# A two-block transformer on one core: conditioning begun three steps sooner, products formed tile by tile behind two norms, and the final norm split in two

## The chip, the core and the metric

The kernel runs on one core of a Trainium2 chip. The metric is the device time of one execution in microseconds (us), shown as the median of three runs. A profile of one execution gives the span from the first to the last instruction and the rows quoted below. Lines such as L823 are those of the kernel before; PE is TensorE, PEld its weight loads, DVE VectorE, ACT ScalarE, POOL GpSimd, SP the queue that issues nearly all DMAs.

## What is computed

Two layers of a first block (three kinds of attention, then a gated FFN) are followed by a second block: an adaptive norm, a mixer of two linear-attention branches over 512 latent and 256 context tokens, a gated FFN, and a last norm. Width is 1024, FFN width 2816, all fp32. What the change touches:

```
mod   = silu(c) @ w_ada + b_ada          # 48 tiles of 128 features; 16 of them for the context too
u     = norm1(x) * (1 + sc1) + sh1       # latent, 512 tokens; u_c likewise for 256 context tokens
q, k, v, low_rank, gate, ... = split(u @ w_in), split(u_c @ w_in)
x     = x + g1 * mixer(...)
h     = norm2(x) * (1 + sc2) + sh2
x     = x + g2 * ((silu(h @ wa) * (h @ wb)) @ w_out)
out   = x * rsqrt(mean(x*x, features) + eps) * final_g
```

## The kernel before

The five engines each run a program written out by hand; semaphores alone order them. The stream `xT` is kept transposed, as 8 tiles of 128 features by 512 tokens. Exact fp32 products are three fp32r products: a value is split into a rounded high part and the rest, and high x high, low x high and high x low are summed in one PSUM bank. So a group over 8 feature tiles is 24 matmuls. ACT makes the high parts of weights and activations, DVE the low parts (POOL in a few places).

**FFN steps.** Each FFN has 38 steps `q` (`ffn`, `load_ffn`, `ffn_silu`, `ffn_sums`). Steps 0 to 21 form one tile of gate and one of up, 48 matmuls; steps 22 to 37 form half of one output tile each, 33 matmuls (the down stage). Weights go through two buffers: SP loads `raws`, ACT rounds it to `wH` (L1792), DVE subtracts to `wL` (L2289). SP issues the load of step `q` when step `q-2` is split.

**Conditioning.** `mod` needs 64 loads of `w_ada`, 32 in each of the first block's two FFNs, one per step from step `ADA_FIRST` = 5 to step 36. For each, SP loads 512 KB into one half of `spare` (L1506) behind the step's weights, and waits first until ACT has read the result before the last. POOL multiplies and folds the tile, PE sums it with two one-column matmuls behind the step's products, and ACT copies the column into `mod` (L1834) behind its split of the step after next. Two loads of the context tokens (L1540) wait for the last two results.

**Start of the second block.** ACT forms the root; DVE spreads it, and makes the 8 tiles of `u` one after another (L2267, L2270, then the low part L2263, with ACT's high part between them). PE first transposes the normed context (L1226), then forms the 32 low-rank rows of `u` tile by tile as the tiles come, and after them q and k of the first head, 24 matmuls each. ACT takes the context's banks between its high parts (L1856, L1857: 16 of them, scale and shift). The context's low parts are on DVE (L2337). Then come the context's low-rank rows, its k, the two decay products, six v tiles and two gate tiles. ACT evacuates in that order; between the decay products and the first v tile it does the decay's logarithms and exponentials, waiting for DVE's sums between them. The banks for these products are a ring of three.

**Second block's FFN.** Its norm is made in the same way. Step 0 forms the gate tile as the 8 tiles come, and then the up tile.

**End.** After the last down step, the squares (summed by POOL) give the mean; ACT takes the root, DVE inverts and spreads it through a matmul, and multiplies the 8 tiles by gain and inverse (L2062). PE transposes them back in 32 pieces (L1462), ACT copies eight banks to SBUF (L608) and issues one DMA of 2 MB.

Of the kernel before, what the change touches and what calls it, by code (L numbers as in the profile page):

```python
# [6 lines left out]
F32 = mybir.dt.float32  # L7
ALU = mybir.AluOpType
# [13 lines left out]
FT = FF // P  # L22
# [59 lines left out]
def build(nc, A, out):  # L82
    ctx = ExitStack()
    with ctx:
# [326 lines left out]
        sc_ready, st_ready = sem("sc_ready"), sem("st_ready")  # L411
        gates_logged = sem("gates_logged")
        og_ready, og_root, og_normed, y_ready = sem("og_ready"), sem("og_root"), sem("og_normed"), sem("y_ready")
        head_in = sem("head_in")
# [187 lines left out]

        def finish_act(act, ap, ab, f):
            ysb = R[:, 14208:14208 + TT * D].rearrange("p (t c) -> p t c", t=TT)
            for t in range(TT):
                for half in range(2):
                    bank = ab.take(act)
                    ap.do(f(ysb[:, t, half * 512:(half + 1) * 512], bank[:, :], ACT.Copy), a_free)  # L608
            act.dma_start(out[0].rearrange("(t p) c -> p t c", p=P), ysb).then_inc(out_done, 16)

# [4 lines left out]
        def _(pool):  # L615
# [187 lines left out]
            first_low(L)  # L803
            fold_squares()


        @block.tensor
        def _(pe):
# [303 lines left out]
            def ffn(l):  # L1112
# [24 lines left out]
                for q in range(NF):  # L1137
# [5 lines left out]
                    else:  # L1143
                        pe.wait_ge(wl_ready, g)
                    if q < FT:
                        for n, b_ in ((0, ab), (1, db)):
                            w = [(lambda k, t=t: t[:, g % 2, (n * KT + k) * P:(n * KT + k + 1) * P]) for t in (wH, wL)]
                            deferred = l < L and n == 0
                            bank = gate_bank(q) if deferred else b_.fill(pe)
                            products(bank[:, :], w, lambda k: xH[:, k, :], xl, list(range(KT)), True, True,  # L1150
                                     (lambda k: pp.more(xn_ready)) if q == 0 and n == 0 else None
                                     ).then_inc(gate_full if deferred else b_.filled, 1)
                            if l < L and q == 0:
                                if n == 0:
# [21 lines left out]
                if l == L - 1:  # L1176
                    folded_sums(PTb[:, 0, :], PTb[:, 1, :])
                elif l == L:
                    folded_sums(X(0), X(KT - 1))
                if l < L:  # L1180
# [38 lines left out]

            spread_roots(S)  # L1220
            pp.more(ctx_ready, CT)
            for kp in range(4):
# [125 lines left out]
            parts_job(ab, lambda b: b[0:32, 0:256], small(LR_AT, 2 * RANK), XcP)  # L1348
            pe.wait_ge(tab_in, 80)
            ranked = ab.n  # L1350
# [104 lines left out]
            ffn(L)  # L1455
            spread_roots(S)
            pp.more(xn_ready, KT)
            for t in range(TT):
                for half in range(2):
                    bank = ab.fill(pe)  # L1460
                    for f in range(4):
                        ins = nc.tensor.transpose(bank[:, f * P:(f + 1) * P], xn[:, half * 4 + f, t * P:(t + 1) * P], ident[:, :])  # L1462
                    ins.then_inc(a_full, 1)


        @block.sync
        def _(sp):
# [91 lines left out]
            load_ffn(L)  # L1559
            sp.wait_ge(out_done, 16)  # L1560


        @block.scalar
        def _(act):
# [229 lines left out]
            def second_ffn_inputs():  # L1794
# [7 lines left out]
                split_high(L, 1)  # L1802

            def ffn_silu(l):
                for q in range(NF):
# [14 lines left out]
                    if q >= FT and (q - FT) % 2:  # L1820
                        k = (q - FT) // 2
                        if l + 1 < L:
                            high_tile(x_high(k), k)
                        if l < L:
                            square_in_turn(k)
                        else:
                            square(k)
                    if l + 1 < L and q == NF - 2:
# [21 lines left out]
            for k in range(KT):  # L1850
                high_tile(x_high(k), k)
                if k % 2 == 0:
                    bank = ab.take(act)
                half = bank[:, k % 2 * 256:(k % 2 + 1) * 256]
# [3 lines left out]
                if k % 2:  # L1858
                    ap.also(ctx_split)

            def rank_rows(a, n):
# [66 lines left out]
            evacuate(0, *[("v", m) for m in range(4)])  # L1928
            evacuate(0, ("v", 4), ("v", 5), ("gate", 0), ("gate", 1))
            for h in range(NH2):  # L1930
# [75 lines left out]
            for n in range(2 * KT):  # L2006
# [4 lines left out]
                ap.also(gate_ready)  # L2011
            second_ffn_inputs()
            ffn_silu(L)
            root()
            finish_act(act, ap, ab, f)


        @block.vector
        def _(dve):
# [198 lines left out]

            def gained(k, gain):
                vp.do(v.tensor_scalar(Pb[:, k % 2, :], xT[:, k, :], gain(k), None, ALU.mult), scaled)  # L2220

# [79 lines left out]
            def ffn_sums(l, add):  # L2301
                for m in range(KT):
# [11 lines left out]
                    if l < L:  # L2314
                        fold(m)

# [15 lines left out]

            norm_into_parts(lambda k: gm[:, 0, k:k + 1], lambda k: mod[:, sh1 + k, 0:1], u_low, x_high, context_root)
            vp.more(ctx_split, KT // 2)
            for k in range(0, KT, 2):
# [5 lines left out]
            vp.do(v.memset(seg[:, 0:SEQ2:CH], 0.0))  # L2341

            def second_low(name, h):
                j = SECOND.index((name, h))
                raw_, high, low = place_parts(PLACE[j])
                dve.wait_ge(second_high, j)
                vp.do(v.tensor_tensor(low, raw_, high.bitcast(F32), ALU.subtract), piece_split)  # L2347

# [57 lines left out]

            second_low("v", 0)
            decay_sums(0, 0)
# [148 lines left out]
            for m in range(KT):  # L2557
# [5 lines left out]
                vp.also(x_ready)  # L2563
            ffn_norm(L, lambda k: gm[:, 2, k:k + 1], lambda k: mod[:, sh2 + k, 0:1])
            ffn_products(L)
# [58 lines left out]
```

## Time and profile before

| | |
|---|---|
| median of 3 runs (lowest, highest) | 2967.97 us (2957.62, 2972.18) |
| profiled execution | 2958.03 us |
| its span | 2956.2 us |
| mean granted TensorE clock in the span | 0.958 of full speed |
| PE busy in the span | 2765.4 us (94%) |
| chain that ended last, by engine | PE 76%, DVE 8%, ACT 7%, DMA 7% |

Times in the rows count from the start of the span. The profiled execution lies at the low end of the three runs. PE holds most of the chain, so the places of interest are those where another engine or a DMA holds it.

### The profile page before, as it was taken

How to read it: one execution, taken by the hardware profiler on the slowest of the kernel's cores; microseconds unless marked ns; L12 is line 12 of the kernel's file. 1: busy time of each engine (PE TensorE's matmuls, PEld its weight loads, DVE VectorE, ACT ScalarE, POOL GpSimd, SP SyncE). 2: the span in 40 equal slices, each digit the busy share in tenths (PEclk: the TensorE clock that was granted, in tenths of full speed). 3: DMA queues.
4: the chain of work that ended last, by engine and by line, in shares of the span. 5: the costliest groups of instructions: out<-in, count | busy, mean ns of one | idle time of the engine just before them, and what ended most of it. 6: DMA issues, size and time to landing. Idle time of an engine off the chain costs nothing.

```text
span 2956.2 us, 35461 instructions
## 1 busy us (share of the span) xinstructions
PE 2765.4 (94%) x13958; PEld 2144.4 (73%) x13958; DVE 1315.1 (44%) x1765; ACT 977.6 (33%) x1648; POOL 900.0 (30%) x664
## 2 busy tenths in 40 slices
PE   7989999999999799999998999898988999899997
PEld 7866658887798575788876776657776665688886
DVE  2758435453345773554424355645443112333322
ACT  5469522222253882222224334332222100222221
POOL 5566402435547551124463100300000322200000
PEclk8999999999999999999999999899987999899999
DMA  5230024554522101345453111011111331233332
GB/s 129 90 69 1 19 57 120 144 141 132 143 84 78 36 1 47 100 117 140 132 148 97 45 43 43 29 43 29 34 39 43 86 85 57 72 100 100 87 88 68
DMA packets 386054, 230.40 MB, mean 78 GB/s; under 512 B 9340, under 2 KB 382204, under 8 KB 385888
## 3 DMA queue, kind: packets, MB, share of 16 engines
q1 hardware_dynamic: 383408, 224.09, 27.5%
q0 software_dynamic: 1952, 1.94, 0.8%
q8 instruction: 111, 1.82, 0.3%
q10 hardware_dynamic: 528, 2.10, 0.2%
q14 instruction: 55, 0.45, 0.0%
HBM read 226.01 MB, written 2.10 MB: 77 GB/s over the span
## 4 chain that ended last, share of the span: by engine, by line
PE 76%; DVE 8%; ACT 7%; DMA 7%; issue 2%; POOL 0%; SPq 0%; ACTq 0%; DVEq 0%; POOLq 0%
PE ps L823 65%; PE scores L823 8%; DMA raws<-in_w_down 5%; PE ps L965 1%; ACT wH L1792 1%; DVE R L2094 1%; DVE ring_parts L2347 1%; DMA ring<-in_w_in 1%; ACT U L1631 0%; ACT spare L1654 0%; ACT R L1919 0%; DMA R<-in_x 0%; DVE R L2267 0%; DVE R L2270 0%; DVE spare L2104 0%
## 5 line engine op out<-in xcount | busy, mean ns | idle before, releaser
L823 PE MATMUL ps<-xH,wH 128*128 128x512 f32 x1000 | 397.3, 397 | 8.2 <-DVE xL L2263 8.2
L823 PE MATMUL ps<-xL,wH 128*128 128x512 f32 x1000 | 391.6, 392 | 0.0
L823 PE MATMUL ps<-xH,wL 128*128 128x512 f32 x1000 | 391.3, 391 | 0.0
L2289 DVE TENSOR_TENSOR wL<-raws,wH 128x2048 fp32r<-128x2048 f32 (+1 forms) x113 | 232.8, 2060 | 283.6 <-ACT wH L1792 283.4
L1792 ACT ACTIVATE wH<-raws 128x2048 fp32r<-128x2048 f32 (+1 forms) x114 | 192.9, 1692 | 500.3 <-PE ps L823 307.5
L823 PE MATMUL ps<-ring_parts,U_parts 128*128 128x256 f32 (+1 forms) x1952 | 320.3, 293 | 21.3 <-DVE ring_parts L2146 6.2
L823 PEld LDWEIGHTS ps<-ring_parts,U_parts 128*128 128x128 f32 x1952 | 285.5, 201 | 36.4 <-issue 29.5
L823 PE MATMUL ps<-R 128*64 128x128 f32 (+6 forms) x1768 | 279.0, 346 | 28.7 <-issue 4.8
L716 POOL TENSOR_TENSOR spare<-spare,cvec 128x1024 f32<-128x1024 f32 x64 | 124.4, 1943 | 560.1 <-DMA spare<-in_w_ada 560.1
L823 PEld LDWEIGHTS ps<-R 128*64 128x64 f32 (+2 forms) x1768 | 173.5, 167 | 132.4 <-issue 77.0
L823 PEld LDWEIGHTS ps<-xH,wH 128*128 128x128 f32 x1000 | 188.9, 189 | 52.8 <-issue 8.5
L823 PE MATMUL ps<-U_parts,ring_parts 128*128 128x512 f32 (+2 forms) x704 | 208.9, 389 | 9.5 <-DVE ring_parts L2347 9.5
L823 PEld LDWEIGHTS ps<-xH,wL 128*128 128x128 f32 x1000 | 188.9, 189 | 39.6
L823 PE MATMUL ps<-R,ring 128*128 128x512 f32 x496 | 216.1, 593 | 1.3 <-DVEq L56 1.3
L823 PEld LDWEIGHTS ps<-xL,wH 128*128 128x128 f32 x1000 | 189.2, 189 | 38.5 <-issue 1.0
L823 PE MATMUL ps<-hH,wH 128*128 128x512 f32 x528 | 209.2, 396 | 1.1 <-DVE wL L2289 1.1
L785 POOL CAST ring_parts<-ring 128x2048 fp32r<-128x2048 f32 x23 | 46.5, 2020 | 527.4 <-DMA ring<-in_w_in 527.2
L823 PE MATMUL ps<-hL,wH 128*128 128x512 f32 x528 | 206.5, 391 | 0.0
L823 PE MATMUL ps<-hH,wL 128*128 128x512 f32 x528 | 206.5, 391 | 0.0
L718 POOL TENSOR_TENSOR spare<-spare 128x512 f32<-128x512 f32 (+2 forms) x192 | 199.3, 1038 | 15.0
L823 PEld LDWEIGHTS ps<-R,ring 128*128 128x128 f32 x496 | 94.0, 190 | 112.9 <-issue 110.3
L823 PEld LDWEIGHTS ps<-U_parts,ring_parts 128*128 128x128 f32 (+1 forms) x704 | 128.7, 187 | 43.5 <-DVE ring_parts L2347 10.4
(404 smaller groups left out, 4616.4 us busy)
## 6 DMA issues: line engine op xcount, KB each, us to landing
raws<-in_w_gate_up SPq DMA_DIRECT2D x88, 512.0 KB, 5.3
ring<-in_w_in SPq DMA_DIRECT2D x34, 1024.0 KB, 5.8
spare<-in_w_ada SPq DMA_DIRECT2D x64, 512.0 KB, 4.0
raws<-in_w_down SPq DMA_DIRECT2D x32, 704.0 KB, 6.1
raws<-in_w_ffn_in SPq DMA_DIRECT2D x44, 512.0 KB, 5.0
ring<-in_w_in SPq DMA_DIRECT2D x22, 512.0 KB, 6.1
raws<-in_w_ffn_out SPq DMA_DIRECT2D x16, 704.0 KB, 4.5
ring<-in_w_o SPq DMA_DIRECT2D x6, 896.0 KB, 5.2
```

The source lines that it names most:

```text
L716: pg.do(nc.gpsimd.tensor_tensor(w_, w_, bc(cvec[:, :, ADA[a][1]], P, 2), ALU.mult))
L718: pg.do(nc.gpsimd.tensor_tensor(w[:, 0:n_ * P], w[:, 0:n_ * P], w[:, n_ * P:2 * n_ * P], ALU.add), ada_summed if n_ == 1 else None)
L785: pg.do(nc.gpsimd.tensor_copy(high, raw_), second_high)
L823: return nc.tensor.matmul(o, a, b, start=first, stop=last)
L965: ins = nc.tensor.transpose(bank[:, s_ * P:(s_ + 1) * P], PX[a % 4][:, c, s_ * P:(s_ + 1) * P], ident[:, :])
L1792: ap.do(f(wH[:, g % 2, 0:n], raws[:, g % 2, 0:n], ACT.Copy), wh_ready)
L2094: vp.do(v.tensor_reduce(nmax[:, n:n + 2], SP[a % 2][:, :, :], AX.X, ALU.max, negate=True), s_max)
L2289: vp.do(v.tensor_tensor(wL[:, g % 2, 0:n], raws[:, g % 2, 0:n], wH[:, g % 2, 0:n].bitcast(F32), ALU.subtract), wl_ready)
L2347: vp.do(v.tensor_tensor(low, raw_, high.bitcast(F32), ALU.subtract), piece_split)
```

## The change

Four edits:

1. `ADA_FIRST` is 2 instead of 5: the conditioning takes steps 2 to 33 of each FFN.
2. At the second block's start, PE forms the low-rank rows, q and k of the first head together: three matmuls of each for every tile as it comes. The context's transposes follow. ACT takes the context's banks after q and k; its high parts of `u` are no longer mixed with them. Two of the latent v tiles (2 and 3) are formed before the context's low-rank rows and k, and the other four after the decay products. DVE's low part of the v weights comes before the context's low parts.
3. Step 0 of the second block's FFN forms gate and up together, tile by tile.
4. The final norm is split: in the down stage, DVE multiplies each finished tile by the gain alone, PE transposes it one step later, ACT copies it into the output buffer `ysb`; its square is summed by DVE in turn. After the root, ACT and DVE multiply the output rows of two token tiles each by the inverse, and SP writes each token tile by a DMA of its own, 512 KB.

```diff
-        ADA_FIRST, N_ADA = 5, len(ADA) // L
+        ADA_FIRST, N_ADA = 2, len(ADA) // L
...
+        FIRST_LAST = [("v", 4), ("v", 5), ("v", 0), ("v", 1), ("gate", 0), ("gate", 1)]
...
-                    if q < FT:
+                    if l == L and q == 0:
+                        w = [[(lambda k, t=t, n=n: t[:, g % 2, (n * KT + k) * P:(n * KT + k + 1) * P]) for t in (wH, wL)] for n in range(2)]
+                        banks = [ab.fill(pe), db.fill(pe)]
+                        for k in range(KT):
+                            pp.more(xn_ready)
+                            both = [products(banks[n][:, :], w[n], lambda k: xH[:, k, :], xl, [k], k == 0, k == KT - 1) for n in range(2)]
...
+                    if l == L and q > FT and (q - FT) % 2 == 0:
+                        pp.more(last_gained)
+                        transposes([Pb[:, ((q - FT) // 2 - 1) % 2, t * P:(t + 1) * P] for t in range(TT)], P)
...
+            pe.wait_ge(lr_split, 1)
+            pe.wait_ge(branch_split, 1)
+            weights_ = small(LR_AT, 2 * RANK), piece_columns(0, 0, P), piece_columns(0, DK, P)
+            rows_out = (2 * RANK, P, P)
+            at_once = [parts_steps(ab.fill(pe)[0:n, :], w, XP) for n, w in zip(rows_out, weights_)]
+            for k in range(KT):
+                pp.more(xn_ready)
+                lasts = [next(steps) for steps in at_once]
...
-            pe.wait_ge(lr_split, 1)
-            parts_job(ab, lambda b: b[0:32, :], small(LR_AT, 2 * RANK), XP, lambda: pp.more(xn_ready))
...
-            for name, m in PROJECTIONS[:2]:
-                run(first(name, m))
+            run(first("v", 2))
+            run(first("v", 3))
...
-            for name, m in PROJECTIONS[3:]:
+            for name, m in FIRST_LAST:
...
-            sp.wait_ge(out_done, 16)
+            for t in range(TT):
+                sp.wait_ge((by_act, by_dve)[t % 2], t // 2 + 1)
+                sp.dma_start(out[0, t * P:(t + 1) * P, :], ysb[:, t, :]).then_inc(out_done, 16)
+            sp.wait_ge(out_done, 16 * TT)
...
+            def tokens_out(m):
+                bank = ab.take(act)
+                ap.do(f(ysb[:, :, m * P:(m + 1) * P], bank[:, :].rearrange("p (t c) -> p t c", t=TT), ACT.Copy), a_free)
+                ap.also(tile_out)
...
+            def context_tiles():
+                for k in range(KT):
+                    if k % 2 == 0:
+                        bank = ab.take(act)
+                    context_tile(k, bank)
...
-            evacuate(0, *PROJECTIONS[:2])
+            evacuate(0, ("q", 0), ("k", 1))
+            context_tiles()
+            evacuate(0, ("v", 2), ("v", 3))
...
-            finish_act(act, ap, ab, f)
+            tokens_out(KT - 1)
+            ap.more(last_inv)
+            for t in range(0, TT, 2):
+                ap.do(f(ysb[:, t, :], ysb[:, t, :], ACT.Copy, scale=rt[:, t:t + 1]), by_act)
...
+                    elif l == L:
+                        if m >= 2:
+                            dve.wait_ge(tile_out, m - 1)
+                        gained(m, lambda k: vec2[:, 2, k:k + 1], last_gained)
...
-            norm_apply(lambda k: vec2[:, 2, k:k + 1])
+            vp.more(root_ready)
+            vp.do(v.reciprocal(rt[:, :], rt[:, :]), last_inv)
+            dve.wait_ge(tile_out, KT)
+            for t in range(1, TT, 2):
+                vp.do(v.tensor_scalar(ysb[:, t, :], ysb[:, t, :], rt[:, t:t + 1], None, ALU.mult), by_dve)
```

On PE at the start of the second block, before: the sums of squares and the spread, the context's transposes, then the low-rank rows alone (32x512).

```order
L856 MATMUL ps<-ones,R 128x1 x8
L823 MATMUL ps<-R,ones 128x512
L1226 MATMUL scores<-ident,spare 128x128 x4
L1226 MATMUL ps<-ident,spare 128x128 x8
L1226 MATMUL scores<-ident,spare 128x128 x4
L823 MATMUL ps<-U_parts,R_parts 32x512
L823 MATMUL ps<-ring_parts,R_parts 32x512
L823 MATMUL ps<-U_parts,R_parts 32x512 x2
```

And now, for the first tile of `u` and the start of the second:

```order
L851 MATMUL ps<-ones,R 128x1 x8
L818 MATMUL ps<-R,ones 128x512
L818 MATMUL scores<-U_parts,R_parts 32x512
L818 MATMUL scores<-ring_parts,R_parts 32x512
L818 MATMUL scores<-U_parts,R_parts 32x512
L818 MATMUL ps<-U_parts,ring_parts 128x512
L818 MATMUL ps<-ring_parts 128x512
L818 MATMUL ps<-U_parts,ring_parts 128x512 x2
L818 MATMUL ps<-ring_parts 128x512
L818 MATMUL ps<-U_parts,ring_parts 128x512
L818 MATMUL scores<-U_parts,R_parts 32x512
```

The transposes have moved behind eight such rounds, and each tile feeds nine matmuls in three banks instead of three in one.

On ACT at the same place, before (L1583 is a high part of `u`, L1856 and L1857 one context tile):

```order
L1583 ACTIVATE U_parts<-R 128x512
L1856 ACTIVATE R<-scores,mod,gm 128x256
L1857 ACTIVATE U_parts<-scores,mod,gm 128x256
L1583 ACTIVATE U_parts<-R 128x512
L1856 ACTIVATE R<-scores,mod,gm 128x256
```

And now (L1641 and L1906 copy out the low-rank rows, q and k):

```order
L1593 ACTIVATE U_parts<-R 128x512 x8
L1641 ACTIVATE R<-scores 32x512
L1906 ACTIVATE R<-ps 128x512
L1641 ACTIVATE R<-ps 128x512
L1871 ACTIVATE R<-scores,mod,gm 128x256
L1872 ACTIVATE U_parts<-scores,mod,gm 128x256
```

All 16 context operations now stand behind the eight high parts and three copies.

On SP at the end of the second layer's FFN, before (`raws` are the down weights, `spare<-in_w_ada` the conditioning, `in_ctx` the context, `ring<-in_w_in` the first weights of the second block):

```order
L1506 DMA spare<-in_w_ada 128x8x128
L1500 DMA raws<-in_w_down 128x11x128
L1506 DMA spare<-in_w_ada 128x8x128
L1500 DMA raws<-in_w_down 128x11x128
L1540 DMA spare<-in_ctx 128x1024 x2
L1531 DMA ring<-in_w_in 128x8x128 x2
```

And now:

```order
L1513 DMA spare<-in_w_ada 128x8x128
L1507 DMA raws<-in_w_down 128x11x128
L1513 DMA spare<-in_w_ada 128x8x128
L1507 DMA raws<-in_w_down 128x11x128 x4
L1547 DMA spare<-in_ctx 128x1024 x2
L1538 DMA ring<-in_w_in 128x8x128 x2
```

The last four weight loads follow each other with no conditioning load between them.

## Rows read from the trace of the kernel before

**Rows 1.** Chain of waits, whole span: start, us, engine, tile, line, count

```profile
435.74 54.44 PE ps L823 x240
...
1268.38 11.01 PE ps L823 x48
1279.51 11.01 PE ps L823 x48
...
1570.77 7.65 PE ps L823 x33
```

**Rows 2.** Timeline of SP's queue: start, us, line, operation; both down stages

```profile
680.33 0.37 SPq L1506 DMA_DIRECT2D spare<-in_w_ada  x1
...
788.35 0.37 SPq L1506 DMA_DIRECT2D spare<-in_w_ada  x1
...
1457.85 0.37 SPq L1506 DMA_DIRECT2D spare<-in_w_ada  x1
...
1560.37 0.37 SPq L1506 DMA_DIRECT2D spare<-in_w_ada  x1
```

**Rows 3.** Timeline of PE, second layer's down stage; in brackets idle time and releaser

```profile
1545.24 0.38 PE L823 MATMUL scores<-ones,spare 128*128 128x1 f32 x2 [1.00 <-POOL spare L718]
```

**Rows 4.** Timeline of DVE, start of the second block

```profile
1588.67 2.26 DVE L2263 TENSOR_TENSOR ring_parts<-R,U_parts 128x512 fp32r<-128x512 f32 x1
...
1602.43 1.48 DVE L2263 TENSOR_TENSOR ring_parts<-R,U_parts 128x512 fp32r<-128x512 f32 x2
1604.39 2.87 DVE L2337 TENSOR_TENSOR spare_parts<-R,U_parts 128x512 fp32r<-128x512 f32 x4 [0.48 <-ACTq L56]
```

**Rows 5.** Timeline of POOL, same stretch

```profile
1588.42 1.97 POOL L785 CAST ring_parts<-ring 128x2048 fp32r<-128x2048 f32 x1
```

**Rows 6.** Timeline of ACT, same stretch

```profile
1584.59 2.33 ACT L1849 ACTIVATE spare<-spare,rsg 128x1024 f32<-128x1024 f32 x2 [0.36 <-DVE rsg L2331]
...
1592.93 0.56 ACT L1856 ACTIVATE R<-ps,mod,gm 128x256 f32<-128x256 f32 x1
```

**Rows 7.** Timeline of PE, first head of the second block

```profile
1621.35 0.69 PE L823 MATMUL scores<-R,C 32*128 32x256 f32 x2
...
1637.29 0.77 PE L823 MATMUL ps<-ring_parts,U_parts 128*128 128x256 f32 x2 [5.57 <-ACT R L1631]
...
1659.61 0.82 PE L1271 MATMUL ps<-ident,R 128*128 128x128 f32 x6
```

**Rows 8.** Windows: length, busy us (instructions) of five engines, granted clock, DMA

```profile
1595.00:1597.00 2.00, 0.71 (x2) 0.35 (x3) 1.90 (x3) 1.76 (x4) 0.00 (x0) 0.50 0.00 0
1604.00:1610.00 6.00, 6.00 (x28) 4.81 (x28) 4.89 (x8) 0.90 (x2) 0.00 (x0) 1.00 0.00 0
2562.00:2566.00 4.00, 3.29 (x7) 1.66 (x7) 3.79 (x7) 1.26 (x2) 0.00 (x0) 0.50 0.60 159
```

**Rows 9.** Timeline of all engines, step 0 of the second block's FFN

```profile
2561.66 0.76 PE L823 MATMUL ps<-xH,wH 128*128 128x512 f32 x1 [6.01 <-DVE xL L2263]
...
2573.01 1.48 DVE L2263 TENSOR_TENSOR xL<-R,xH 128x512 fp32r<-128x512 f32 x2
...
2575.67 2.29 DVE L2289 TENSOR_TENSOR wL<-raws,wH 128x2048 fp32r<-128x2048 f32 x1 [1.18 <-ACT wH L1792]
...
2582.22 1.92 ACT L1792 ACTIVATE wH<-raws 128x2048 fp32r<-128x2048 f32 x1 [3.57 <-PE ps L823]
```

**Rows 10.** Timeline of all engines, behind the last down step

```profile
2930.18 0.95 PE L856 MATMUL scores<-ones,U 128*128 128x1 f32 x8
...
2933.52 0.18 DVE L2051 RECIPROCAL rt<-rt 128x4 f32<-128x4 f32 x1 [2.32 <-ACTq L56]
...
2949.24 0.42 ACTq L609 DMA_DIRECT2D out_x<-R  x1
```

**Rows 11.** DMA issues: line's tiles, queue, count, KB each, median us to landing

```profile
out_x<-R ACTq DMA_DIRECT2D x1, 2048.0 KB, 6.6
...
spare<-in_ctx SPq DMA_DIRECT2D x2, 512.0 KB, 4.2
```

More of the change, by code:

```diff
@@ L412, in build @@
         gates_logged = sem("gates_logged")
+        last_gained, tile_out, by_act, by_dve, last_inv = sem("last_gained"), sem("tile_out"), sem("by_act"), sem("by_dve"), sem("last_inv")
         og_ready, og_root, og_normed, y_ready = sem("og_ready"), sem("og_root"), sem("og_normed"), sem("y_ready")
@@ L601, in permute @@
                 pg.do(e.tensor_copy(part, scratch))
[L603 to L609, printed above, removed]
+        ysb = U[:, :, :].rearrange("p a c -> p (a c)")[:, 0:TT * D].rearrange("p (t c) -> p t c", t=TT)
         block = ctx.enter_context(nc.Block())
@@ L803, in _ @@
             first_low(L)
-            fold_squares()
         @block.tensor
@@ L1144, in ffn @@
                         pe.wait_ge(wl_ready, g)
-                    if q < FT:
+                    if l == L and q == 0:
[4 more added lines that the diff above has]
+                            both = [products(banks[n][:, :], w[n], lambda k: xH[:, k, :], xl, [k], k == 0, k == KT - 1) for n in range(2)]
+                        both[0].then_inc(a_full, 1)
+                        both[1].then_inc(d_full, 1)
+                        f_by.append((d_full, db.n))
+                    elif q < FT:
                         for n, b_ in ((0, ab), (1, db)):
@@ L1173, in ffn @@
                             f_by.append((d_full, db.n))
+                    if l == L and q > FT and (q - FT) % 2 == 0:
+                        pp.more(last_gained)
+                        transposes([Pb[:, ((q - FT) // 2 - 1) % 2, t * P:(t + 1) * P] for t in range(TT)], P)
                     if ada_at(l, q) is not None:
                         modulation(ada_at(l, q))
-                if l == L - 1:
+                if l >= L - 1:
                     folded_sums(PTb[:, 0, :], PTb[:, 1, :])
-                elif l == L:
-                    folded_sums(X(0), X(KT - 1))
                 if l < L:
@@ L1220, in _ @@
             spread_roots(S)
+            pe.wait_ge(lr_split, 1)
[6 more added lines that the diff above has]
+                lasts = [next(steps) for steps in at_once]
+            for ins in lasts:
+                ins.then_inc(a_full, 1)
             pp.more(ctx_ready, CT)
@@ L1344, in _ @@
             first = projections(0)
-            for name, m in PROJECTIONS[:2]:
-                run(first(name, m))
+            run(first("v", 2))
+            run(first("v", 3))
             pp.more(xn_ready, KT // 2)
             parts_job(ab, lambda b: b[0:32, 0:256], small(LR_AT, 2 * RANK), XcP)
+            ranked = ab.n
             pe.wait_ge(tab_in, 80)
-            ranked = ab.n
             run(first("k", 0))
@@ L1455, in _ @@
             ffn(L)
[L1456 to L1463, printed above, removed]
+            pp.more(last_gained)
+            transposes([Pb[:, (KT - 1) % 2, t * P:(t + 1) * P] for t in range(TT)], P)
         @block.sync
@@ L1823, in ffn_silu @@
                             high_tile(x_high(k), k)
[L1824 to L1827, printed above, removed]
+                        if l == L and k > 0:
+                            tokens_out(k - 1)
+                        square_in_turn(k)
                     if l + 1 < L and q == NF - 2:
@@ L1851, in _, with context_tile @@
                 high_tile(x_high(k), k)
-                if k % 2 == 0:
-                    bank = ab.take(act)
+            def context_tile(k, bank):
                 half = bank[:, k % 2 * 256:(k % 2 + 1) * 256]
@@ L1927, in _ @@
             decay_exponents(0, 0)
-            evacuate(0, *[("v", m) for m in range(4)])
-            evacuate(0, ("v", 4), ("v", 5), ("gate", 0), ("gate", 1))
+            evacuate(0, *FIRST_LAST)
             for h in range(NH2):
@@ L2012, in _ @@
             second_ffn_inputs()
+            turns += 1
             ffn_silu(L)
             root()
-            finish_act(act, ap, ab, f)
+            tokens_out(KT - 1)
+            ap.more(last_inv)
+            for t in range(0, TT, 2):
+                ap.do(f(ysb[:, t, :], ysb[:, t, :], ACT.Copy, scale=rt[:, t:t + 1]), by_act)
         @block.vector
@@ L2217, in layer, with gained @@
                 ffn_sums(l, lambda m, bank: vp.do(v.tensor_tensor(xT[:, m, :], xT[:, m, :], bank[:, :], ALU.add), d_free))
-            def gained(k, gain):
-                vp.do(v.tensor_scalar(Pb[:, k % 2, :], xT[:, k, :], gain(k), None, ALU.mult), scaled)
+            def gained(k, gain, ready=scaled):
+                vp.do(v.tensor_scalar(Pb[:, k % 2, :], xT[:, k, :], gain(k), None, ALU.mult), ready)
             def fold(k):
@@ L2313, in ffn_sums @@
                         low_x(m)
-                    if l < L:
-                        fold(m)
+                    fold(m)
             for l in range(L):
@@ L2333, in _, with second_low @@
             norm_into_parts(lambda k: gm[:, 0, k:k + 1], lambda k: mod[:, sh1 + k, 0:1], u_low, x_high, context_root)
+            def second_low(name, h):
+                j = SECOND.index((name, h))
+                raw_, high, low = place_parts(PLACE[j])
+                dve.wait_ge(second_high, j)
+                vp.do(v.tensor_tensor(low, raw_, high.bitcast(F32), ALU.subtract), piece_split)
+            second_low("v", 0)
             vp.more(ctx_split, KT // 2)
@@ L2341, in _ @@
             vp.do(v.memset(seg[:, 0:SEQ2:CH], 0.0))
[L2343 to L2347, printed above, removed]
             def decay_sums(h, d):
@@ L2405, in head_outputs @@
                 vp.also(y_ready)
-            second_low("v", 0)
             decay_sums(0, 0)
@@ L2564, in _ @@
             ffn_norm(L, lambda k: gm[:, 2, k:k + 1], lambda k: mod[:, sh2 + k, 0:1])
+            squares += KT
             ffn_products(L)
```

## The prediction

> **What bounds the kernel now.** I read the chain of waits first, then the timelines where it leaves PE, then the windows for the clock. PE holds 76% of the chain (table above), so the change can only pay where PE waits or runs slowly. There are four such places, one for each edit.
>
> In the down stages a step's 33 matmuls take 33 x 54.44/240 = 7.5 us at full clock: 240 matmuls took 54.44 us, 0.2268 each [rows 1]. But in layer one the last 13 conditioning loads went out from 680.33 to 788.35, 12 steps of 9.00 us; in layer two the last 13 from 1457.85 to 1560.37, 12 steps of 8.54 [rows 2]. Conditioning sets that pace: PE waits on POOL's sum [rows 3], and SP, standing at a conditioning load that waits for ACT's read, issues the next weights late. The reader should see that the only down step without conditioning behind its weights, the last, runs at once: 7.65 us, its last matmul's tail included [rows 1].
>
> At the second block's start and in step 0 of its FFN, PE follows DVE's tiles. Between the ends of the first low part (1590.93) and of the seventh (1603.17, the row holds two) lie 6 x 2.04 us [rows 4]; three matmuls need a third of that, and the granted clock there is 0.50, the lower of its two levels (1.2 GHz) [rows 8]. Behind the last product, at 2930.2, 26.0 us pass in which PE has little to do [rows 10].
>
> **Edit 1, conditioning three steps sooner.** Nothing is added: 64 loads, sums and matmuls remain. Three of them in each layer move from down steps to up steps. The down steps 34 to 36 lose 9.00 - 7.49 and 8.54 - 7.49 us: 3 x 1.51 + 3 x 1.05 = 7.7. Three up steps each get what an up step with conditioning costs: 1279.51 - 1268.38 = 11.13 against 54.44/5 = 10.89, so 6 x 0.24 = 1.4 [rows 1]. An up step covers the load and POOL's sum, being PE's own length. Gain 6.2. If the weights' own transfer sets the pace without conditioning too, it is -1.4; the cover missing in the first up steps would cost more, but steps 5 to 21 ran with the same queue order. At most 7.7. On SP the context's loads and the first weights are no longer behind a conditioning result, so they land sooner and POOL splits them sooner. POOL's cast of the next weights overlaps the first low part, which took 2.26 us where the last two took 0.74 each [rows 4, 5]; moved ahead, it gives that tile 1.5 us (bounds 0 and 1.5).
>
> **Edit 2, the second block's start.** PE's clock is low at its beginning, so I count the first tile's nine matmuls at twice 0.2268: 4.1 us. From then on PE works without a gap and I take full clock: it was 0.50 at 1595 to 1597, where PE had been waiting, and 1.00 at 1604 to 1610, where it worked without a gap [rows 8]. Nine matmuls are then 2.04 us, just DVE's pace, so the first tile's delay stays. First tile 1590.93 - 1.5 = 1589.4; end of low-rank rows, q and k at 1589.4 + 4.1 + 7 x 2.04 = 1607.8. Before, q and k, 24 x 0.2268 = 5.4 each, came behind the low-rank rows.
>
> But the context has moved too. ACT copies three banks (0.6 each, the last after 1607.8), then does 16 context operations of 0.56, with the gap 0.6: 1608.4 + 9.6 = 1618.0. Then DVE's four low parts, 2.87 and a short wait: 1621.2 [rows 4, 6]. PE's transposes and two v tiles (24 half-width matmuls, 2.7 each) run beside that. Then the context's low-rank rows and k, 2.7 each: the decay products start at 1626.6. Before they started at 1621.35 [rows 7]: 5.3 later. In return two v tiles, 5.4, no longer stand behind them. The wait of 5.57 us before the fourth v, while ACT is held by the decay [rows 7], stays. Gain 0.1, call it 0.2. Queued behind these waits are ACT's evacuations and with them the ring of three banks; the gates' low part on DVE stands behind the decay as before. Bounds: if ACT and DVE were hidden, PE alone would need 1607.8 + 16 transposes at 0.82/6 + 4 x 2.7 = 1620.8, gain 6; if the waits left the context's products at the lower clock, 5.4 more, loss 5.2.
>
> **Edit 3, step 0 of the last FFN.** First tile ready at 2561.6. Six matmuls are 2.7 us at the lower level, 1.4 at the full one, and tiles come every 2.04. Two tiles at the lower level, continuous: 2567.1; then PE waits for tiles again. The last low part ends at 2574.5, the products at 2575.9. Next, step 1 needs its low weights: 2575.67 + 2.29 = 2577.96 [rows 9]. That is late next. Step 0 ended at 2582.2 (ACT's rounding then waited for it). Gain 4.2. At the lower level throughout it would end at 2561.6 + 8 x 2.72 = 2583.4: -1.2. No more than 4.2.
>
> **Edit 4, the end.** Added on PE: seven times four transposes in the down stage, where PE is busy throughout. Six took 0.82 [rows 7], so four are 0.5 and all 3.5. DVE's and ACT's additions (gain, fold, copy, square per 15 us pair of steps) lie beside PE. After the last product the root's way is unchanged up to the inverse, 2933.7 [rows 10]. Beside it PE transposes the last tile and ACT copies it: about 2934.7. Then two scalings each on ACT and DVE, 2.33/2 = 1.17 on ACT [rows 6] and taken equal on DVE: 2937.0. The first DMA goes out at about 2936, the last at 2937.4. By the last one alone, 4.2 us for 512 KB, it lands at 2941.6; by the bytes, 6.6 for 2 MB from the first, 2942.6 [rows 11]. I take the later, and the 0.4 between landing and span's end as before (2949.24 + 6.6 against 2956.2): 2943.0. What goes: 2956.2 - 2943.0 = 13.2, less 3.5: gain 9.7. Bounds: 13 if the transposes hid, -0.6 if the four ran one after another (2936 + 16.8 + 0.4).
>
> The trace has one store only, of 2 MB, 6.6 us, and 512 KB as loads, 4.2 [rows 11]; so a quarter of the bytes takes well over a quarter of the time. The Trainium skill, "DMA: Bandwidth & Descriptors" (Anatomy of one DMA), gives each DMA a fixed cost of about 2.0 us beside bytes at 436 GB/s. Its estimates, 6.8 and 3.2 us, agree with the first row and are 1.0 below the second; it speaks against the split only if the fixed parts don't overlap.
>
> **Sum.** 6.2 + 0.2 + 4.2 + 9.7 = 20.3. Against the profiled execution: 2958.03 - 20.3 = 2937.7. That execution is 9.9 below the median. The four known executions average 2963.95, 5.9 above it, and I add that: 2943.6.
>
> **Rivals.**
> Weights set the down stage's pace, not conditioning. For: DMA has 7% of the chain. Against: the last down step's weights went out right behind the last conditioning load, at 1560.37, and it started 10 us later and ran at full pace [rows 1, 2]. Edit 1 then gives -1.4, the total 12.7: 2945.3 in the profile's terms, 2951.2 expected.
>
> The four stores run one after another. For: no row shows stores overlapping. Against: the one store moved four times the bytes in 1.6 times as long [rows 11], so the parts that don't grow with size would have to stand in line four times. Edit 4 gives -0.6, the total 10.0: 2948.0, or 2954.
>
> Step 0 of the last FFN stays at the lower clock to its end, and only there: edit 3 gives -1.2, the total 14.9: 2943.1, or 2949. For it speaks the 0.50 at 2562 to 2566 [rows 8]; against it that six matmuls fill the time where three didn't.
>
> Slower: PE stays at the lower clock from the first tile of `u` to the first head's gates. Place: second block's start. Price: the joint group 72 x 0.2268 = 16.3 - 2.0 = 14.3 more, the context's rows and k 5.4, three v tiles 8.1 less the 5.57 of wait, the fourth v 2.7 and two gates 10.9: 35.8. With edit 3 at -1.2 the total is 6.2 + 0.2 - 35.8 - 1.2 + 9.7 = -20.9: 2978.9, or 2985. It decides once the lost time there passes 20 us, so only if the level holds past the decay products. For: there are now gaps of ACT's making behind the joint group. Against: the clock was at 1.00 where PE worked without gaps [rows 8], and its own gaps before the decay products are under 3 us each by the times above. The Trainium skill, "TensorE: Matmul & The Clock Gate" (HAM oscillation), says that a kernel whose PE waits again and again between bursts pays the lower clock each time. By that rule this rival would hold; the trace agrees for step 0 and not for the first head.
>
> **Numbers.** Forecast 0.70, weights 0.08, stores 0.08, step 0 0.10, slow clock 0.04. The range takes in a gain of 27 (edits 1 and 2 at their upper ends) from the fastest executions, 2931, and one of 11 to 12 from a run at the old median, 2957. About 0.5%, 15 us, is what a measurement here can tell from no change. Faster by more: most of the forecast, half of step 0, a third of weights and a little of stores, 0.78; within, 0.18; slower, 0.04, the slow clock.
>
> **What would show it.** Edit 1: conditioning loads end at step 33, and steps 34 to 37 take 7.5 us each in both layers. Edit 2: nine matmuls per tile at 2.04 us after the first; decay products 5 us later against the norm's first tile, the first head's gates ending where they did. Edit 3: step 1 starts right behind its low weights, about 16.4 us after the first tile. Edit 4: the span ends 12.8 us after the last product. Wrong would be: down steps above 8 us without conditioning, a clock of 0.50 after the joint group, or stores landing more than 7 us after the first was issued.

## The result, and the profile after

The changed kernel takes 2935.1 us (median of four, 2931.78 to 2940.23) against 2966.35 (four, 2957.62 to 2972.18) of the kernel before: ratio 0.9906, 95% interval 0.9884 to 0.9928, so 28 us less (21 to 34). The forecast was 2943.6 us, a gain of 20.3. The profiled execution took 2931.78 us, its span 2930.0, 26.2 less than before. Lines below are those of the changed kernel.

The chain of waits, as in [rows 1] (start, us, what):

```profile
770.97 30.27 PE ps L818 x132
...
1542.43 30.07 PE ps L818 x132
...
2566.09 5.76 PE scores L818 x24
```

Each down stage now ends with four steps in one piece, 7.5 us each; before, only the last ran so. The conditioning loads, SP's timeline, as in [rows 2]:

```profile
636.50 0.37 SPq L1513 DMA_DIRECT2D spare<-in_w_ada  x1
647.63 0.37 SPq L1513 DMA_DIRECT2D spare<-in_w_ada  x1
658.22 0.37 SPq L1513 DMA_DIRECT2D spare<-in_w_ada  x1
669.35 0.37 SPq L1513 DMA_DIRECT2D spare<-in_w_ada  x1
...
760.49 0.37 SPq L1513 DMA_DIRECT2D spare<-in_w_ada  x1
```

The last now goes out at 760.49, not at 788.35. SP issued the first four 11.13, 10.59 and 11.13 us apart; what an up step takes is read on PE. From the first product of layer one's FFN to its first down product, before:

```profile
421.57 0.79 PE L823 MATMUL ps<-xH,wH 128*128 128x512 f32 x1
...
668.18 0.48 PE L823 MATMUL ps<-hH,wH 128*128 128x512 f32 x1
```

and now:

```profile
420.25 0.79 PE L818 MATMUL ps<-xH,wH 128*128 128x512 f32 x1
...
667.63 0.48 PE L818 MATMUL ps<-hH,wH 128*128 128x512 f32 x1
```

That is 246.6 us with 17 conditioning steps and 247.4 with 20 (the same two lengths in layer two): an up step takes 0.25 us longer with conditioning than without. The second block's start on DVE, as in [rows 4] (start, us, line, tiles, shapes):

```profile
1580.13 0.83 DVE L2296 TENSOR_SCALAR R<-R,mod 128x512 f32<-128x512 f32 x1
1581.00 0.75 DVE L2293 SCALAR_TENSOR_TENSOR R<-xT,gm,ps 128x512 f32<-128x512 f32 x1
1581.78 0.49 DVE L2296 TENSOR_SCALAR R<-R,mod 128x512 f32<-128x512 f32 x1
1582.30 0.69 DVE L2289 TENSOR_TENSOR ring_parts<-R,U_parts 128x512 fp32r<-128x512 f32 x1
```

The first low part takes 0.69 us, not 2.26. The context on ACT, as in [rows 6], first and last of sixteen:

```profile
1602.98 0.56 ACT L1871 ACTIVATE R<-scores,mod,gm 128x256 f32<-128x256 f32 x1
...
1612.21 0.57 ACT L1872 ACTIVATE U_parts<-scores,mod,gm 128x256 fp32r<-128x256 f32 x1
```

PE there and at step 1 of the last FFN, as in [rows 7, 9]: the last of the context's transposes and the first v tile, each behind a wait for ACT to read a bank, the context's low-rank rows, the decay products, the wait for ACT, step 0 and step 1.

```profile
1605.39 0.66 PE L1241 MATMUL scores<-ident,spare 128*128 128x128 f32 x4 [1.74 <-ACT U_parts L1872]
1607.96 0.47 PE L818 MATMUL ps<-ring_parts,U_parts 128*128 128x256 f32 x2 [1.91 <-ACT U_parts L1872]
...
1615.85 0.30 PE L818 MATMUL scores<-U_parts,R_parts 128*32 128x256 f32 x1 [0.43 <-DVE spare_parts L2374]
...
1621.65 0.69 PE L818 MATMUL ps<-R,C 32*128 32x256 f32 x2
...
1636.63 0.77 PE L818 MATMUL ps<-ring_parts,U_parts 128*128 128x256 f32 x2 [4.60 <-ACT R L1641]
...
2549.71 0.76 PE L818 MATMUL ps<-xH,wH 128*128 128x512 f32 x1 [6.01 <-DVE xL L2289]
...
2566.09 0.50 PE L818 MATMUL scores<-xH,wH 128*128 128x512 f32 x1 [1.26 <-DVE wL L2315]
```

Step 1 begins 16.38 us after the first tile's products, behind its low weights. The windows, as in [rows 8] (stretch, us, busy of PE, PEld, DVE, ACT and POOL, granted clock, DMA share, GB/s):

```profile
1584.00:1588.00 4.00, 4.00 (x11) 2.69 (x10) 3.79 (x7) 1.26 (x2) 0.00 (x0) 0.50 0.00 0
1588.00:1592.00 4.00, 4.00 (x18) 2.88 (x17) 3.79 (x7) 1.26 (x2) 0.00 (x0) 0.94 0.02 4
1592.00:1596.00 4.00, 4.00 (x19) 2.86 (x18) 3.75 (x6) 1.27 (x2) 0.00 (x0) 1.00 0.00 0
...
1609.00:1612.00 3.00, 3.00 (x17) 3.00 (x16) 0.00 (x0) 2.75 (x6) 0.00 (x0) 0.50 0.00 0
1616.00:1622.00 6.00, 6.00 (x50) 5.63 (x49) 1.68 (x3) 0.56 (x2) 0.00 (x0) 1.00 0.01 3
...
2552.00:2558.00 6.00, 5.91 (x21) 4.46 (x20) 5.68 (x10) 1.90 (x3) 0.00 (x0) 0.79 0.03 7
2558.00:2566.00 8.00, 6.08 (x24) 4.02 (x23) 6.54 (x8) 4.94 (x5) 0.00 (x0) 1.00 0.00 0
```

In both places the clock rises while the norm's tiles still come. Between them it fell to 0.50 again at 1609 to 1612, behind the two waits for ACT shown above. The end, as in [rows 10, 11]: scaling on ACT and DVE, the four stores.

```profile
2921.87 2.33 ACT L2041 ACTIVATE U<-U,rt 128x1024 f32<-128x1024 f32 x2
2921.90 1.54 DVE L2603 TENSOR_SCALAR U<-U,rt 128x1024 f32<-128x1024 f32 x2 [0.59 <-ACTq L56]
2923.04 2.91 SPq L1569 DMA_DIRECT2D out_x<-U  x4
```

The last product ends at 2917.94, the span 12.1 us later (before 25.9).

**Where the 26.2 us lie.** "The gates" below is the time from the block's first sum of squares on PE to ACT's first copy of the first head's gate. Before:

```profile
1578.24 0.95 PE L856 MATMUL ps<-ones,R 128*128 128x1 f32 x8
...
1654.82 0.60 ACT L1876 ACTIVATE R<-ps 128x512 f32<-128x512 f32 x1
```

and now:

```profile
1572.32 0.95 PE L851 MATMUL ps<-ones,R 128*128 128x1 f32 x8
...
1647.92 0.60 ACT L1897 ACTIVATE R<-ps 128x512 f32<-128x512 f32 x1
```

Up to that copy edits 1 and 2 gave 6.9 (5.9 of it ahead of the sums; the gates fell from 76.6 to 75.6), edit 3 4.0, the rest of the FFN and the end 10.3. That leaves 5.0 in the second block's heads, which no edit touches: between the q products of the last head and the branches they fell by 5.2 (139.9 to 134.7). The experiments begin with that.

### The profile page after: what moved, and what is told of

Same layout as the page of the kernel before. It is cut to its first block, busy times and chain, and to the rows that moved or that the text cites. A ratio compares the mean times of both kernels' runs of the same rounds, so it can differ in the third digit from the quotient of the medians.

```text
span 2930.0 us, 35486 instructions
## 1 busy us (share of the span) xinstructions
PE 2748.7 (94%) x13956; PEld 2132.4 (73%) x13956; DVE 1306.0 (45%) x1772; ACT 980.5 (33%) x1650; POOL 874.1 (30%) x658
## 4 chain that ended last, share of the span: by engine, by line
PE 78%; DVE 8%; ACT 7%; DMA 5%; issue 2%; POOL 0%; SPq 0%; DVEq 0%; ACTq 0%; POOLq 0%
PE ps L818 66%; PE scores L818 8%; DMA raws<-in_w_down 4%; PE ps L960 1%; DVE R L2120 1%; ACT wH L1802 1%; DVE ring_parts L2368 1%; DMA ring<-in_w_in 1%; DVE spare L2130 0%; ACT U L1641 0%; ACT R L1940 0%; DVE QK_parts L2110 0%; DVE wL L2315 0%; ACT spare L1664 0%; ACT R L1641 0%
## 5 line engine op out<-in xcount | busy, mean ns | idle before, releaser
L818 PE MATMUL ps<-U_parts,ring_parts 128*128 128x512 f32 (+2 forms) x720 | 216.2, 391 | 9.5 <-DVE ring_parts L2368 9.5
L714 POOL TENSOR_TENSOR spare<-spare 128x512 f32<-128x512 f32 (+2 forms) x192 | 186.6, 972 | 15.1
```

The source lines that it names most:

```text
L714: pg.do(nc.gpsimd.tensor_tensor(w[:, 0:n_ * P], w[:, 0:n_ * P], w[:, n_ * P:2 * n_ * P], ALU.add), ada_summed if n_ == 1 else None)
L818: return nc.tensor.matmul(o, a, b, start=first, stop=last)
```

## The experiments

**Each edit alone.** `e1_cond`, `e2_second`, `e3_step0` and `e4_final` are the kernel before with one edit of the diff above; in short:

```
e1  ADA_FIRST, N_ADA = 2, len(ADA) // L
e2  FIRST_LAST, at_once, context_tiles, second_low("v", 0) ahead
e3  if l == L and q == 0: gate and up together
e4  gained / transposes / tokens_out, rows scaled, four stores
```

> The kernel before with the first edit alone (conditioning from step 2). The whole change gained 26.2 us of span in the profiled execution: read off both traces 5.9 lie in the two down stages, 1.0 at the second block's start, about 5.0 in that block's heads, which no edit touches, 4.2 in step 0 of its FFN and 10.1 behind the last product. Theory A: each edit gains what stands in its place, and the 5.0 in the heads is the clock's phase, which differs from execution to execution. Then this kernel gains 5.9, ratio 0.998, and from the first products of the second block to the first of its FFN its span is that of the kernel before within 6 us either way. Theory B: the earlier conditioning itself puts the heads into a better phase of the clock. Then it gains about 11, ratio 0.996, and the heads are 5 shorter here.

> The kernel before with the second edit alone (second block's start). Theory A: its place is worth 0.2 as predicted and 1.0 as read off the trace; without the first edit the low part of the first tile still runs beside the cast, so 0 to 1, ratio 1.000 within 0.002. Theory B, that this edit is what shortens the heads: 5 to 6, ratio 0.998, with a higher granted clock from the eighth head on.

> The kernel before with the third edit alone (gate and up of step 0 of the last FFN together). Theory A: step 1 starts right behind its low weights, 4.2 us, ratio 0.9986, and nothing earlier in the program changes. Rival: step 0 stays at the lower clock and the gain is 0 or -1.2.

> The kernel before with the fourth edit alone (final norm split). Theory A: 13.6 us less behind the last product, 3.3 more in the down stage for seven groups of transposes: 10.1, ratio 0.9966, span's end 12.1 us behind the last product. Rival, that the tail's gain is partly given back because the down stage's steps wait for the copies: under 7 us, with pairs of steps above 15.5 us.

Ratios: 0.9971 (0.9960 to 0.9982), 1.0008 (0.9993 to 1.0022), 0.9989 (0.9976 to 1.0002), 0.9960 (0.9944 to 0.9976). In us: 8.6 less, 2.4 more, 3.3 less, 11.9 less; e2 and e3 can't be told from nothing by time alone. By its profile `e2_second` loses at its own place, where 0 to 1 us of gain was expected: its gates are at 79.0, against 77.1 on average of before, e3 and e4. The profiles cut the program at the same PE instructions, in us:

| kernel | layer 1 FFN and on | layer 2 FFN | second block | FFN to step 1 | step 1 to end |
|---|---|---|---|---|---|
| before | 526.6 | 370.9 | 971.0 | 32.7 | 374.2 |
| e2_second | 527.7 | 373.4 | 975.5 | 32.7 | 375.3 |
| e3_step0 | 525.5 | 371.9 | 975.9 | 28.8 | 374.2 |
| e4_final | 526.2 | 372.7 | 974.8 | 32.7 | 363.7 |
| e1_cond | 520.7 | 370.3 | 971.8 | 32.7 | 375.4 |
| after | 522.6 | 369.0 | 965.0 | 28.8 | 363.9 |
| w_all | 522.1 | 370.0 | 972.2 | 28.8 | 363.8 |
| w_no2 | 522.1 | 369.9 | 979.4 | 28.8 | 363.9 |

(The first two columns begin at the up tile of step 0 of that layer's FFN. The ends are: a group of 24 matmuls in the next layer; the second block's sums of squares; those of its FFN; step 1; the span's end.) By the columns' means edit 1 is worth 4.6 and 2.5, edit 3 3.9, edit 4 10.9, and each shows only where it stands. The second block's column can't be read so: before, e3 and e4 run the same instructions there and differ by 4.9.

**The whole again, and without edit 2.** `w_all` is the changed kernel unaltered, `w_no2` has edits 1, 3 and 4.

```
-            run(first("v", 2))
-            run(first("v", 3))
+            for name, m in PROJECTIONS[:2]:
+                run(first(name, m))
... (the rest of edit 2 undone likewise)
```

> The changed kernel once more, unaltered. The four edits alone had ratios 0.9971, 1.0008, 0.9989 and 0.9960, product 0.9928, or 21.3 us; the whole change had 0.9906 of only four executions, 27.9. Theory A: the edits add up, and the rest is the clock's scatter. Then more executions give a ratio of 0.992 to 0.993, and the second block, from its norm's sums to those of its FFN 965.0 us in the first profile, comes out several us longer here (968 to 976) from the same instructions. Theory B: the edits help one another. Then the ratio stays at 0.990 to 0.991 and the block at 965 within 2.

> The changed kernel without its second edit (the second block starts as before). Alone that edit had 1.0008. Theory A: it gains nothing beside the others either, and this kernel is within 2 us of the changed one. Theory B: it pays once the first edit has moved the cast from the first tile, since only then does the joint group run at nine matmuls per tile from the beginning; then this kernel is 5 to 7 us slower than the changed one.

`w_all`: 2937.17 us, ratio 0.9908 (0.9889 to 0.9927). `w_no2`: 2938.21 us, 0.9912 (0.9894 to 0.9930), 1.2 us apart by the ratios, as theory A has it. With intervals of 0.002 either side the times alone don't exclude theory B's 5 to 7; the gates speak against it at the block's start: 74.9 and 76.1 without edit 2 (`w_no2`, `e1_cond`), 75.6 to 76.3 with it. Of `w_all`'s expectation one half came true for each theory: the ratio stayed at 0.991, not 0.992 to 0.993, and yet the second block took 972.2 us. The parts' product, 0.9928, has an error of its own, about 0.003 by the four intervals together, so it can't be told from either.

The stretch from the last head's q products to the branches, changed kernel's first profile (same columns as the windows above):

```profile
2158.32:2293.02 134.70, 121.02 (x545) 93.39 (x545) 55.34 (x133) 29.75 (x54) 10.51 (x4) 0.82 0.12 32
```

And of `w_all`, the same kernel:

```profile
2156.64:2296.60 139.96, 126.28 (x544) 98.77 (x544) 55.39 (x133) 29.76 (x54) 10.28 (x4) 0.80 0.11 31
```

5.3 us more, all of it PE's busy time; DVE and ACT agree to 0.1, and PE is idle for 13.68 us in both. In before, e1 to e4, `w_no2`, `w_onestore` and `z_ada0` the stretch takes 139.7 to 140.0. So the 5.0 us in the heads differ between executions of one kernel, with the granted clock (0.82 against 0.80), and are luck of the profiled one, not the change. The stretch is short too in the four kernels that come below with DVE's copies or unused products (132.2 to 134.8); whether those favour it, one profile of each can't say.

**The context's sixteen operations.** `w_dvectx` has ACT take each context tile once; DVE rounds it:

```
-                ap.do(f(ctx_high_part(k), half, ACT.Identity, bias=shift, scale=gain), ...)
+            for k in range(0, KT, 2):
+                vp.more(ctx_split)
+                vp.do(v.tensor_copy(UP[:, k:k + 2, 0:256], ctxT[:, k:k + 2, :]))
```

> The changed kernel with half of the context's work moved: ACT only takes the eight context tiles from PSUM, and DVE, idle there, makes the eight rounded copies, two tiles an instruction. In the changed kernel ACT's sixteen operations end at 1612.8, DVE's low parts at 1615.8 and the decay products start at 1621.65. If these sixteen set the decay's start, ACT ends 4.8 us sooner, DVE's last copy comes 0.5 later, and the decay products start 4 us sooner (5.4 after the low parts), the first head's gates likewise up to what the three v tiles behind them need. Then the whole gains 2 to 4 us, ratio 0.989 to 0.992. If PE's own two v tiles set the start instead, nothing moves.

Its last rounded copy and low parts on DVE:

```profile
1606.19 0.43 DVE L2372 CAST U_parts<-R 128x512 fp32r<-128x512 f32 x1 [0.85 <-ACTq L56]
1606.65 2.87 DVE L2375 TENSOR_TENSOR spare_parts<-R,U_parts 128x512 fp32r<-128x512 f32 x4
```

and its decay products on PE:

```profile
1615.37 0.69 PE L818 MATMUL ps<-R,C 32*128 32x256 f32 x2
```

From the block's sums they start 5.1 us sooner (44.2 against 49.3), the gates 5.3 (70.3 against 75.6). So ACT's sixteen operations do set the decay's start, as the prediction had it. 2927.95 us, 0.9884 (0.9864 to 0.9904): more than expected, but its profile too has the short stretch, 134.8, and against `w_all` the intervals overlap. ACT holds PE here through the banks as well as through the low parts: PE's two waits for a bank, 1.74 and 1.91 us in the changed kernel, are 0.54 and 0.72, and the two v tiles behind them run at full clock.

**One store.** `w_onestore`:

```
+            sp.wait_ge(by_act, TT // 2)
+            sp.wait_ge(by_dve, TT // 2)
+            sp.dma_start(out[0].rearrange("(t p) c -> p t c", p=P), ysb).then_inc(out_done, 16)
```

> The changed kernel with one store of 2 MB from SP behind all four scalings, in place of four of 512 KB. The four went out from 2923.04 to 2924.8 and landed at 2929.6: 6.6 us from the first, as long as the one store of the kernel before. Theory A: the bytes set it, the four overlap fully, and splitting saves only the time between the first and the last scaling. Then one store goes out 1.2 us later and the span ends 13.3 us behind the last product in place of 12.1. Rival: the four stood in line in part, and one store is as fast or faster: 12.1 or less.

From the last product to the span's end 13.3 us against 12.1: 1.2 more, as theory A has it, in one execution (2940.26 us). One store of 2 MB landed 6.6 us after its issue, the four 6.6 us after the first; splitting the store is a small part of edit 4.

**Unused products in three waits.** `z_fill`:

```
+                    if name == "q" and h > NH2:
+                        for _ in range(14):
+                            mm(bank[:, :], x_high(0)[:, 0:P], x_high(0), True, True)
```

> The changed kernel with work added that nobody uses: ahead of the wait for the low weights of q in three later heads of the second block (waits of 4.40, 3.63 and 3.63 us, behind which the products begin at the lower clock and stay there for 3.7 to 5 us) PE forms 14 products, 3.2 us at full clock, into the bank that q then overwrites. If the scatter of the second block is the clock that falls in such waits, the q products begin at 1.00, each of the three places gains 1.9 to 2.5 us, and the whole 4 to 8 us, ratio about 0.989; the block's PE time falls by that. If the clock doesn't follow these waits, PE only has 10 us more to do inside its waits, and the time is that of the changed kernel within 2 us, or up to 10 us more where the added products run at the lower clock.

The first microseconds of q in the three heads:

```profile
1986.80:1991.00 4.20, 4.20 (x19) 3.47 (x20) 3.69 (x10) 0.00 (x0) 2.17 (x1) 1.00 0.04 13
2076.90:2081.00 4.10, 4.10 (x18) 3.37 (x19) 1.59 (x1) 0.00 (x0) 1.90 (x1) 1.00 0.00 0
2161.70:2165.70 4.00, 3.96 (x17) 3.27 (x18) 2.15 (x1) 0.00 (x0) 1.75 (x1) 1.00 0.00 0
```

and in the changed kernel:

```profile
1985.10:1989.30 4.20, 4.20 (x10) 3.33 (x11) 3.69 (x10) 0.00 (x0) 2.12 (x1) 0.50 0.04 12
2076.50:2080.60 4.10, 4.08 (x11) 3.25 (x12) 1.92 (x1) 0.00 (x0) 1.90 (x1) 0.57 0.01 4
2158.30:2162.30 4.00, 3.98 (x10) 3.17 (x11) 2.17 (x1) 0.00 (x0) 1.73 (x1) 0.55 0.00 0
```

Seventeen to nineteen matmuls in place of ten or eleven: PE's own idleness there brings it to 1.2 GHz, and work in the wait keeps it at 2.4. The time doesn't show it: 2934.27 us, 0.9896 (0.9875 to 0.9916), not to be told from the changed kernel.

**Conditioning from step 0, and sums of the gains.** `z_ada0` is the changed kernel with the first line, `z_best` adds the copies of `w_dvectx`, `z_all` the unused products too.

```
-        ADA_FIRST, N_ADA = 2, len(ADA) // L
+        ADA_FIRST, N_ADA = 0, len(ADA) // L
```

> The changed kernel with conditioning from step 0 in place of 2. By the first edit's terms: two more down steps in each layer fall from 9.05 and 8.65 to 7.5 us, two more up steps rise by 0.24: 3.1 + 2.3 - 1.0 = 4.4 less, ratio 0.989 to 0.990. Rival, that the first up steps have no room for the loads (behind the stage's first weights): 0 or a loss, and PE waits in steps 0 and 1.

> The changed kernel with DVE making the context's rounded copies (as in the run before, ratio 0.9884) and conditioning from step 0. If both add up: 5.6 at the second block's start and 4.4 in the down stages less than the changed kernel, ratio 0.987. If the earlier conditioning gives nothing: 0.9885.

> The changed kernel with all three: DVE's rounded context copies, conditioning from step 0, and the 14 unused products ahead of q in three heads. In the profiles the copies moved the first head's gates by 5.6 us and the unused products brought three stretches of 4.0 to 4.2 us from a granted clock of 0.50 to 0.57 to 1.00, about 2 us each. If the 6 us add to the copies' gain: ratio 0.9845 to 0.986. If the clock elsewhere in the block takes them back, it is that of the run without them, 0.9865 within 0.0015.

`z_ada0`: 2938.11 us, 0.9907 (0.9885 to 0.9929): nothing. Its chain has the last six steps in one piece:

```profile
755.23 46.65 PE ps L818 x198
```

7.77 us a step, not 7.5: 1.7 us more than 198 products of 0.2268. PE waits for nothing in them; their clock is low at first, behind a wait for POOL's sum:

```profile
754.85 0.38 PE L818 MATMUL scores<-ones,spare 128*128 128x1 f32 x2 [2.21 <-POOL spare L714]
```

```profile
757.00:759.00 2.00, 2.00 (x6) 1.61 (x5) 1.89 (x3) 0.41 (x2) 0.00 (x0) 0.50 0.85 250
```

So the first of the six takes 9.2 us and only the other five 7.5; in layer two the same follows a wait of 1.85 us. In the changed kernel's two down stages these waits stay under 1.4 us in the last conditioning steps, and the clock is 1.00 behind them. The up stage is 0.45 longer (247.8 against 247.4 us). In layer one the down stage with the pieces behind it is only 0.3 shorter, in layer two 0.7 longer (282.7 against 283.0; 130.06 against 129.32). Holding the clock up behind that wait was not tried. `z_best`: 2925.93 us, 0.9865 (0.9843 to 0.9888), the fastest of all, 12 us below `z_ada0` beside it, though the intervals still meet; so the copies pay again. In its layer two the wait for POOL's sum is 1.0 us, the clock stays at 1.00 and the down stage takes 128.4 us, not the 130.2 of `z_ada0`. The ratio is the one expected if both add up, yet `z_ada0` alone gave nothing; the interval takes in 0.9885 too. `z_all`: 2932.28 us, 0.9878 (0.9859 to 0.9897; two executions at 2922, three at 2932 to 2934): the unused products did not add up.

## Why the prediction was right, point by point

**Edit 1: the mechanism and both terms right.** Conditioning set the down pace, four steps run at 7.5, and the weights' rival is gone. The up steps cost what was put in for them: 0.75 us a layer by the rows above, 1.5 in all where 6 x 0.24 = 1.4 was said. The stages show 4.6 + 2.5 = 7.1 after that cost, in place of 6.2, so the down steps gave about 8.6 in place of 7.7. The cover for the first low part, taken at 1.5, is 2.2: from the sums to its end 13.2 us on average in the four kernels without edit 1, 11.0 in six with it. By the gates 1.5 of that is left (77.1 on average of three kernels without edits 1 and 2, 75.5 of two with edit 1 and without edit 2).

**Edit 2: right within a microsecond, though its clock was wrong.** In before's time less the 5.9 of edit 1, the joint group should end at 1601.9; the transposes behind it began at 1602.09. The context operations should end at 1612.1; they ended at 1612.78. Against the norm's first tile (DVE's first operation on it) the decay products came 5.5 us later (predicted about 5; 6.2 against the sums), and the gates 1.0 sooner (predicted 0.2) with edit 1's cover in it. Two claims of full clock failed. Behind the first tile it was 0.50 until 1588, so the second tile's first matmuls came 0.43 us apart in place of 0.23. That cost some 0.7 us, since PE ran without a gap from there to the end of the group, while DVE was done with its tiles at 1595.99. And a clock of 0.50 after the joint group, which the prediction had named as a sign of being wrong, did come, at 1609 to 1612: the two waits for banks that ACT had yet to read were not in the sum. The two v tiles took 7.5 us, not 5.4, at no cost here: PE still waited 0.43 us for DVE's low parts.

**Edit 3: right.** 4.0 by the rows (3.9 in the columns), step 1 16.38 us after the first products where 16.4 was said. The clock rose in the middle of the tiles; the rival of step 0 at the lower level is refuted.

**Edit 4: right, 1.2 short.** A pair of steps takes 15.44 us from one to the next where its 66 products take 15.0: the seven groups of transposes cost 3.4, as 3.5 said (119.8 us from the first down product to the end of the last before, 123.2 now). The first store went out 5.1 us after the last product, not 5.8, and the span ended 7.0 us behind it, as 6.6 for the bytes and 0.4 have it; the four didn't stand in line. The fit quoted from the Trainium skill, "DMA: Bandwidth & Descriptors" (Anatomy of one DMA), is given there for DMAs issued by GpSimd; these went out from SP, and overlapped. 10.9 in place of 9.7: 0.7 is the earlier first store, the rest the end of the kernel before, 26.4 us on average of four profiles.

**The sum.** 7.1 + 1.5 - 0.4 (edit 2 beside edit 1: gates at 75.9 on average of three kernels, against 75.5) + 3.9 + 10.9 = 23.0, in place of 20.3: 1.2 more by edit 4, 0.9 by edit 1, 0.9 at the second block's start, 0.3 less by edit 3. The rest of the 27 to 28 us measured is not located. The second block differs by 5 to 9 us between profiles that run the same instructions there (965.0, 972.2 and 974.0 in after, `w_all` and `w_onestore`), and the parts' own ratios allow 21. At the gates edits 1 and 2 help each other: edit 2 costs 1.9 us without edit 1 (one profile) and 0.4 with it. Whether the edits help one another beyond that stays open.

**The slow-clock rival.** It did not happen: the clock was 1.00 at 1592 to 1596 and again at the decay products. But the prediction read the trace wrong where it took the first head to be free of the lower clock behind waits. Before the change too the clock was low there, around the wait of 5.57 us [rows 7]:

```profile
1635.00:1641.00 6.00, 3.71 (x17) 3.74 (x18) 4.63 (x4) 2.83 (x6) 0.00 (x0) 0.50 0.00 0
```

## What to carry to other kernels

A step's length is to be read from the engine that does it, first product to first product: SP's issues alternated between 11.13 and 10.59 us while PE's steps kept their length. An earlier start has an end: from step 0 the last conditioning steps waited longer for POOL, and a stretch at the lower clock behind that wait took much of the gain back. Before a difference in a stretch that no edit touches is explained, compare that stretch in two profiles of the same kernel; here the first profile held 5 us of luck. A join of products is limited by what feeds and follows it, here ACT's sixteen context operations: splitting those over two engines gave what the join itself did not.

## What was not expected

The same 545 matmuls took 121.0 or 126.3 us of PE time in two executions of one kernel, with equal work and waits elsewhere. Three stretches brought from 0.50 to 0.57 up to 1.00 did not shorten the whole measurably: a gain of clock at one place need not remain at the end.
